# Two heads per round in a prompt attention, and the last six rounds of a bisection moved among the products of the next projection

## What is computed

```python
def mixer_ab(hn, attend, conv_buf, h0, w_in, w_out, ...):
    q, k, v, qi, ki, wi, g, xr = split_cols(hn @ w_in, AB_SPLITS)
    attn = attend(q, k, v, qi, ki, wi)                    # prompt: 4 blocks of 128 queries, 8 heads
    rg, new_buf, h_last = rglru_branch(g, xr, conv_buf, h0, ...)
    return jnp.concatenate([attn, rg], axis=-1) @ w_out, ...

# sample attention: the 256 best of 4097 keys by the indexer's scores, for each of 8 samples
idx, valid = select_topk(indexer_scores(qi, wi, ki_all), q_pos, k_pos, 256)
k_sel = jnp.where(in_past, ck[phys, off], ...)            # gathered from a paged cache
# recurrence: h = a * h + u with a = exp(log_a), u = sqrt(-expm1(2 * log_a)) * (i * xc)
```

## Time and profile before

| | |
|---|---|
| median of 3 runs | 1317.52 us (1314.84 to 1319.84) |
| the profiled execution's own time | 1317.3 us |
| its span, first to last instruction | 1315.6 us |
| busy: TensorE, weight loads, VectorE, ScalarE, POOL | 96%, 92%, 53%, 35%, 14% of the span |
| bisection with attention, first count to first product of the output projection | 208.84 to 277.94 us |
| output projection, to the last product | to 367.94 us |

### The profile page before, as it was taken

The page is one execution under the profiler, slowest core; times in us unless marked ns, Lnnn a source line. Parts: engine busy times, 40 slices in busy tenths (PEclk is TensorE's granted clock), DMA queues, the critical chain, the costliest instruction groups (busy, mean ns, idle before and its releaser), DMA issues.

```text
span 1315.6 us, 24604 instructions
## 1 busy us (share of the span) xinstructions
PE 1258.2 (96%) x10078; PEld 1215.9 (92%) x10078; DVE 701.9 (53%) x1286; ACT 465.9 (35%) x540; POOL 187.3 (14%) x281
## 2 busy tenths in 40 slices
PE   6999998888999999999999999999999999999995
PEld 5979994677999999999999999998999999999994
DVE  5468997765265555555323346535655555542223
ACT  5242327642143433434222244333543434331110
POOL 1001101234031111111000010042211111110000
PEclk9999999998999999999999999999999999999998
DMA  6654212022022222222222231211222222222211
GB/s 218 173 115 159 97 33 79 3 101 92 1 105 97 92 96 96 96 96 88 89 89 99 96 129 65 97 66 64 97 96 96 90 74 91 96 88 92 95 53 65
DMA packets 26595, 120.40 MB, mean 92 GB/s; under 512 B 7880, under 2 KB 9224, under 8 KB 14504
## 3 DMA queue, kind: packets, MB, share of 16 engines
q1 hardware_dynamic: 21784, 107.67, 23.8%
q0 software_dynamic: 2048, 10.54, 2.4%
q10 hardware_dynamic: 2704, 1.35, 0.3%
HBM read 115.94 MB, written 3.61 MB: 91 GB/s over the span
## 4 chain that ended last, share of the span: by engine, by line
PE 90%; DVE 6%; issue 2%; ACT 2%; POOL 0%; DMA 0%; another core or an unknown queue 0%; DVEq 0%; SPq 0%; ACTq 0%
PE ps L852 22%; PE ps L855 21%; PE ps L853 21%; PE ps L983 4%; PE ps L984 3%; PE ps L986 3%; PE ps L1250 2%; PE ps L932 2%; PE ps L1251 1%; PE ps L1253 1%; PE ps L869 1%; PE ps L916 1%; DVE xc L1498 1%; PE ps L1054 1%; PE ps L897 1%
## 5 line engine op out<-in xcount | busy, mean ns | idle before, releaser
L852 PE MATMUL ps<-xh,w_h 128*128 128x260 f32 x1664 | 437.5, 284 | 7.4 <-POOL xl L2001 7.4
L853 PE MATMUL ps<-xl,w_h 128*128 128x260 f32 x1664 | 436.0, 283 | 0.0
L855 PE MATMUL ps<-xh,w_l 128*128 128x260 f32 x1664 | 335.3, 283 | 0.0
L852 PEld LDWEIGHTS ps<-xh,w_h 128*128 128x128 f32 x1664 | 315.1, 189 | 8.3 <-issue 7.6
L853 PEld LDWEIGHTS ps<-xl,w_h 128*128 128x128 f32 x1664 | 314.5, 189 | 0.1
L1353 DVE TENSOR_TENSOR w_l<-w_raw,w_h 128x2048 fp32r<-128x2048 f32 (+1 forms) x94 | 212.7, 2263 | 160.1 <-ACT w_h L519 159.9
L855 PEld LDWEIGHTS ps<-xh,w_l 128*128 128x128 f32 x1664 | 257.3, 189 | 0.0
L519 ACT ACTIVATE w_h<-w_raw 128x2048 fp32r<-128x2048 f32 (+1 forms) x50 | 92.3, 1845 | 263.3 <-PE ps L855 213.4
L853 PE MATMUL ps<-hl,w_h 128*128 128x260 f32 x704 | 183.9, 282 | 0.0
L852 PE MATMUL ps<-hh,w_h 128*128 128x260 f32 x704 | 183.4, 282 | 0.0
L855 PE MATMUL ps<-hh,w_l 128*128 128x260 f32 x704 | 141.8, 283 | 0.0
(11 more groups left out here) (311 smaller groups left out, 1569.4 us busy)
## 6 DMA issues: line engine op xcount, KB each, us to landing
w_raw<-in_wstream SPq DMA_DIRECT2D x86, 1024.0 KB, 4.8
w_raw<-in_wstream SPq DMA_DIRECT2D x8, 768.0 KB, 4.4
res<-in_x_t SPq DMA_DIRECT2D x4, 520.0 KB, 7.1
out_y<-yt SPq DMA_DIRECT2D x8, 260.0 KB, 2.2
tab<-bias_by_distance SPq DMA_DIRECT2D x16, 128.0 KB
wor<-in_wstream SPq DMA_DIRECT2D x4, 512.0 KB, 6.0
wm<-in_sgu_w ACTq DMA_DIRECT2D x1, 512.0 KB, 3.6
sb_b<-in_sgu_b ACTq DMA_DIRECT2D x1, 512.0 KB, 4.1
```

The lines of the kernel that those rows point to most:

```text
L852: pe.matmul(out[h], wh, hi[h], start=(first and k == 0), stop=False)
L853: pe.matmul(out[h], wh, lo[h], start=False, stop=False)
L855: ins = pe.matmul(out[h], wl, hi[h], start=False, stop=(last and k == nk - 1))
```

## The change

It changes only orders. (1) Heads 16 to 31 have their logits two per round, in rounds 17 to 24. (2) `rg_share` moves to rounds 4 to 7, the square root to the place ahead of all exponentials, the scans to rounds 13 to 16, `rg_samples` to 17, `fill_high` to 21 to 24. (3) The split of slab 11 moves to round 14 on ScalarE and to round 20 on VectorE. (4) TensorE's counts of rounds 26 to 31 move behind steps 0, 2, 3, 5, 7 and 9 of the first slab (`LATE_ROUNDS`), with the last values at step 0, the last output transposes at 4, and everything of the selection and the sample attention some steps later. (5) On VectorE the last division comes after round 27, `attention_low` after round 30, the first slab's `add_half` ahead of the slot ranks' inputs, and the slot rows, `add_half` and the split of slab 12 are ordered anew.

```diff
-        for rnd in range(17, 33):
-            ROUND[rnd] = (rnd - 1,)
+        for rnd in range(17, 25):
+            ROUND[rnd] = (2 * rnd - 18, 2 * rnd - 17)
...
             act.wait_ge(ex_done, 4)
             act.wait_ge(th_done, 4)
-            act.wait_ge(slab_done, 10)
-            split(11, 1)
+            act.wait_ge(e_done, 4)
+            act.activation(th[:], th[:], ACT.Sqrt).then_inc(sqrt_done, 1)
...
-                if rnd == 17:
-                    roots()
-                if 29 <= rnd < 33:
-                    fill_high(1, rnd - 29, gg[:, rnd - 29, :], rg_done, rnd - 28)
+                if rnd == 14:
+                    act.wait_ge(slab_done, 10)
+                    split(11, 1)
+                if 21 <= rnd < 25:
+                    fill_high(1, rnd - 21, gg[:, rnd - 21, :], rg_done, rnd - 20)
...
-            for rnd in range(32):
+            for rnd in range(26):
                 count(rnd)
...
-                if n == 1:
+                if n == 0:
+                    p_work(26)
+                if n in LATE_ROUNDS:
+                    count(LATE_ROUNDS[n])
+                if n == 4:
+                    p_out(NCH - 1)
+                if n == 12:
                     tie_counts()
-                if n == 2:
-                    p_work(33)
-                if n == 4:
+                if n == 15:
                     chosen_before()
-                if n == 5:
-                    p_work(34)
-                if n == 7:
+                if n == 18:
                     for i in range(3):
                         slot_ranks(i)
-                    p_out(NCH - 1)
-                if 8 <= n < 21:
-                    slot_ranks(n - 5)
+                if 19 <= n < 32:
+                    slot_ranks(n - 16)
...
-                if n == 56:
+                if n == 60:
                     sample_rows()
...
-            p_work(32)
+            LATE_ROUNDS = {0: 26, 2: 27, 3: 28, 5: 29, 7: 30, 9: 31}
...
                 compare(rnd)
-                if 9 <= rnd < 13:
-                    rg_share(rnd - 9)
-                if rnd == 13:
+                if 4 <= rnd < 8:
+                    rg_share(rnd - 4)
+                if rnd == 8:
                     dve.wait_ge(e_done, 4)
                     dve.memset(atr[:, :, SEQ:T], 0.0)
+                if rnd == 20:
                     split(11, 1)
-                if 21 <= rnd < 25:
-                    rg_scan(rnd - 21)
-                if rnd == 25:
+                if 13 <= rnd < 17:
+                    rg_scan(rnd - 13)
+                if rnd == 17:
                     rg_samples()
...
                 decide(rnd)
+                if rnd == 27:
+                    p_divide(NCH - 1)
+                if rnd == 30:
+                    for j in range(4):
+                        attention_low(j)
...
-            p_logits(31)
...
+            add_half(0, 0)
+            add_half(0, 1)
             dve.wait_ge(base_mm, 1)
...
-            p_divide(NCH - 1)
...
-            for i in range(3):
+            for i in range(9):
                 slot_row(i)
-            for j in range(4):
-                attention_low(j)
-            for i in range(3, 11):
+            split_next(10)
+            slot_row(9)
+            add_half(1, 0)
+            for i in range(10, 16):
                 slot_row(i)
-            add_half(0, 0)
-            add_half(0, 1)
-            for i in range(11, 16):
-                slot_row(i)
+            add_half(1, 1)
             hot_buckets()
-            split_next(10)
-            add_half(1, 0)
-            add_half(1, 1)
```

More of the change, by code:

```diff
@@ L1188, in beside_out @@
                 n = 16 * g + step
-                if n == 1:
+                if n == 0:
[5 more added lines that the diff above has]
+                if n == 12:
                     tie_counts()
-                if n == 2:
-                    p_work(33)
-                if n == 4:
+                if n == 15:
                     chosen_before()
-                if n == 5:
-                    p_work(34)
-                if n == 7:
+                if n == 18:
                     for i in range(3):
                         slot_ranks(i)
-                    p_out(NCH - 1)
-                if 8 <= n < 21:
-                    slot_ranks(n - 5)
-                if n == 24:
+                if 19 <= n < 32:
+                    slot_ranks(n - 16)
+                if n == 34:
                     keys_turn(0)
-                if n == 25:
+                if n == 35:
                     hot_turn()
-                if n == 29:
+                if n == 37:
                     keys_turn(1)
-                if n == 31:
+                if n == 38:
                     sample_logits(0)
-                if n == 37:
+                if n == 44:
                     keys_turn(2)
-                if n == 44:
+                if n == 49:
                     keys_turn(3)
-                if n == 45:
+                if n == 50:
+                    sample_logits(1)
+                if n == 51:
                     weights_turn(0)
-                if n == 46:
-                    sample_logits(1)
-                if n == 47:
+                if n == 52:
                     sample_values(0)
-                if n == 51:
+                if n == 55:
                     weights_turn(1)
-                if n == 53:
+                if n == 57:
                     sample_values(1)
-                if n == 56:
+                if n == 60:
                     sample_rows()
@@ L1676, in p_divide, with attention_low, add_half @@
                    sumr[:, blk, :].rearrange("p (h a) -> p h a", a=1).broadcast_to((P, 8, 64)), ALU.mult).then_inc(ao_done, 1)
+            def attention_low(j):
+                dve.wait_ge(at_ev, NCH)
+                dve.wait_ge(x_lo, 12)
+                dve.wait_ge(x_hi, 13 + j)
+                tt(xl[:, 4 + j, :], atr[:, j, :], xh[:, 4 + j, :].bitcast(F32), ALU.subtract).then_inc(x_lo, 1)
+            def add_half(g, t):
+                dve.wait_ge(half_done if t == 0 else slab_done, 10 + g + 1)
+                for h in range(2):
+                    r = res[:, 2 * g + t, h * HT:(h + 1) * HT]
+                    ins = tt(r, ps[:, 2 * t + h, 0:HT], r, ALU.add)
+                ins.then_inc(half_added if t == 0 else b_free, 1)
             key_halves()
@@ L1747, in slot_row @@
                     tt(row2[:, four], grow[:, four], gab[:, four, 0], ALU.add).then_inc(rows2_done, 1)
-            def attention_low(j):
-                dve.wait_ge(at_ev, NCH)
-                dve.wait_ge(x_lo, 12)
-                dve.wait_ge(x_hi, 13 + j)
-                tt(xl[:, 4 + j, :], atr[:, j, :], xh[:, 4 + j, :].bitcast(F32), ALU.subtract).then_inc(x_lo, 1)
             def hot_buckets():
@@ L1761, in hot_buckets @@
                 tt(hot_b[:], dge[:, :, 1:33], dge[:, :, 0:32], ALU.subtract).then_inc(hot_done, 1)
-            def add_half(g, t):
-                dve.wait_ge(half_done if t == 0 else slab_done, 10 + g + 1)
-                for h in range(2):
-                    r = res[:, 2 * g + t, h * HT:(h + 1) * HT]
-                    ins = tt(r, ps[:, 2 * t + h, 0:HT], r, ALU.add)
-                ins.then_inc(half_added if t == 0 else b_free, 1)
             def sample_least(n):
```

3 lines of the change are left out of this document (removed).

## The result

The changed kernel takes 1329.2 us (median of 4 runs, 1326.5 to 1331.4); the kernel before took 1318.4 beside it. The ratio is 1.0085, its 95% interval 1.0064 to 1.0106: slower, where the forecast was 1310.5. The profiled execution, the longest of the four (1331.4), spans 1329.6 us, 14.0 more than before.

The account below looks back on a forecast made before the run. TensorE, nine tenths of the chain of waits, was taken as the bound. Gains of 2.9, 0.4 and 5.3 make 8.6, less 1.7 for half clock: 1317.3 - 6.9 = 1310.4, say 1310.5 us; range 1303 to 1319.

Parts of the forecast that it names:

- the term of the table load: Rounds 4 to 9: the root's own load, bounds 0 and 1.28 us, taken as 0; head 0's exponential 2.3 late.
- two terms of the sum: Rounds 10 to 16: some 5.5 us from head 0's exponential to head 8's logits; scan waiting for rates, head 8 1.6 late.
- VectorE is the bound at 2.5 per round: Rounds 10 to 16 after head 8: VectorE sets the pace, 2.5 us per round, 4.4 in round 15.
- the waits of the divisions: Rounds 17 to 25: divisions of blocks 1 and 2 ahead of logits, with round 20's split, leave TensorE 2.5 us idle.
- The first slab: Output projection's first slab: waits 10.9 us before, 5.05 after, counts 0.6, so 5.3 gained.
- The rest: Gathers of keys, samples' output rows and SyncE's slab loads move at no cost; 1 to 2 us without cover.
- The signal with no engine behind it: End of the first slab: VectorE's 2.35 us standing, within the 4.48 wait, let go; its return kept as a bound.
- The wait at the key turns: Behind the first slab: a wait at the key turns was named as a sign that the forecast is wrong.
- POOL: Rounds 10 to 13: its multiplication slows threshold updates, up to 0.6 us in each of three rounds; taken as 0.
- C: Rival: new waits keep TensorE at 1.2 GHz from step 3 to 23 of the projection; 1323.2, up to 1326; chance 0.12.
- B: Rival, gain eaten: root's load waits (1.28), the 2.35 returns, one more half-clock stretch (1.5); 1315.5 us; chance 0.16.
- D: Rival: pair rounds stay a three-engine loop, about 4.7 us each, eight rounds; slab gains as forecast; 1317.4 us; chance 0.08.

Follow-up runs that it names:

- i1: h2 with the root back in round 17, shares in rounds 9 to 12 and scans behind the logits in rounds 20 and 21; 1314.7 us.
- h2: g2 without its filling products in rounds 4 to 13 (those of the changed kernel stay); 1309.9 us, ratio 0.9942 to the kernel before.
- g2: f2 with g1's order, the hot turn a step later and filling products (results thrown away) in rounds 4 to 13; 1312.5 us.
- f2: The changed kernel with e2's later scans and e3's wait ahead of the ninth gather together; 1315.9 us.
- g1: The changed kernel with the divisions of blocks 0 to 2 and VectorE's half of slab 11's split behind the logits and decision; 1326.0 us.
- f1: The changed kernel with more products whose result is thrown away, in TensorE's gaps of rounds 4 to 13; 1326.9 us.
- e2: The changed kernel with the four scans in rounds 17 to 20, the samples' step in 21 and the fills two rounds later; 1322.5 us.
- e3: The changed kernel with POOL waiting for the hot buckets ahead of the ninth gather; 1322.4 us.

## Why the prediction was wrong

**Rounds 4 to 9: the term of the table load.** The last share ended 9.6 us after the first count, as forecast. The root's own load I put at the lower of its bounds, 0, and it took the upper, 1.28: it stands behind the wait for the shares in ScalarE's order, though ScalarE had been idle 3.15 us. Head 0's exponential at 221.71 looks like the forecast's 221.7, but this execution's loop began 1.36 earlier; it is 1.4 late. By the Trainium skill, ScalarE: Activation LUTs, section "What ACT_TABLE_LOAD costs", 1.38 us of drain were to come with each load; as before, none shows (root 0.01 us after the load, load 0.02 after the root).

**Rounds 10 to 16: two terms of the sum.** I took 5.5 us from head 0's exponential to head 8's logits without the split and the shares. With the split gone, i1 has 7.4, and h2, without shares or scans in these rounds, 8.9 (7.95 in g2, where the clock stays full): most of what I subtracted from the 8.66 had been hidden. The scan's wait for the rates then came on top, at 24.7 after the first count instead of 19.8, and "VectorE is the bound at 2.5 per round" failed with it: the scan is ahead of the logits in a loop over three engines. The place was right (the prediction named the wait), its size was not: head 8 was 6.5 late where I had 1.6.

**Rounds 17 to 25: the waits of the divisions.** TensorE is the bound, as forecast, and its work without waits is 33.2 us from head 16's logits (h2), where I had 30.7 (0.9, 29.4 and 0.4). For the divisions and the split I took 2.5; f2 against h2 shows 3.55, since a late second head also runs by itself, 0.91, instead of together with the first. Block 2's division brought half clock besides (0.72 over 6 us), and with it g1 against the changed kernel shows 4.8.

**The first slab: right.** Waits of 0.78, 0.99, 0.54 and 0.91 for the forecast 1.05, 1.15, 0.9 and 1.05, at full clock, so even the 1.0 set aside for half clock was not needed.

**The rest: the step that failed most.** The gathers were costed at nothing, 1 to 2 us without cover. By the profiles they cost 9 to 10 (99.2 against 90.1 and 88.8), by the medians 6.8 to 11.3, with the half clock behind them; where that ended sooner the same sixteen gathers left 93.5 (f1). The cover that I looked at was not what failed: the first gather was issued 13.7 us ahead of the first turn of keys, 8.6 closer than before where I had 3, and the turn did not wait for it. What failed is that the gathers were put down as transfers alone, at no cost to the other engines. The signal with no engine behind it was in the rows, and so were the gathers before, which had pauses; I treated it as part of a wait that would go, with its 2.35 us as the bound. ScalarE's timeline of the kernel before has the same sign:

```profile
303.14 1.91 ACT L519 ACTIVATE w_h<-w_raw 128x2048 fp32r<-128x2048 f32 x1 [12.89 <-remote]
```

This split could start when the first slab was done, at about 300.1. It and the slot row at 303.18 both began within 0.2 us of the end of the eighth gather in a row (303.06). The wait at the key turns that I named as a sign came (0.36, and 1.59 at the hot turn). With slot rows that now come without a pause, the gathers lost theirs.

**POOL** beside rounds 10 to 13: a threshold update took 0.70 where POOL multiplied, and ScalarE was awaited there anyway; 0 was right.

**The rivals.** C gave the sign and came nearest to the time, by a mechanism that did not happen: the clock in the slab stayed full from 283.8 to 324. B's load came true. Of D's eight rounds of 4.7, three lasted about that long or longer. No rival had the gathers in it. With the same work done, taking out one loss does not bring the run back into the range: it is at 1322.5 with the scans later (e2) and at 1322.4 with the pause (e3). With both it is at 1315.9 (f2). That h2's 1309.9 is close to the forecast is partly luck: it is another kernel, still has the table load's 1.4, and its two stretches (67.5 and 86.7) lie 1.3 above and 0.8 under the 66.2 and 87.5 of the sum.

## What to carry to other kernels

In a loop over several engines, work that nobody awaits in the same round belongs behind the step that others wait for; costed as filling an engine's spare time, it is paid again as a late partner on the engine that sets the pace. A wait that the profile puts down to no engine is a cost to place, not one to drop: ask which stream of transfers runs beside it and what the change does to that stream's pauses. Before filling gaps to hold up a clock, see whether the stretch at the lower level is on the path at all.

## What the runs showed of the hardware

Sixteen indirect gathers in a row (0.95 us each, 0.3 apart, 21 us in all) kept ScalarE from an instruction that was ready for 8.6 us, and it went on 1.8 to 2.2 us after the last one's issue in four kernels; a pause of 6.1 us in the middle, or plain loads of the same size with pauses of 1.2 to 3.7 us, removed that. Eight in a row were felt too: 3.0 us on ScalarE and 2.35 on VectorE in the kernel before, 0.91 on VectorE in e3. By the Trainium skill, Runtime: NRT & Kernel Launch, section "Instruction fetch mechanics", each sequencer fetches its instructions in blocks of 16 KiB over a DMA queue of its own, mostly hidden; this trace has such a queue (43 packets with 0.70 MB, 16 KB each), but no run here shows that it was a fetch that the gathers held. Between 318 and 340 us the changed kernel moved one packet on it, in the microsecond from 323, and none near 331.8, when ScalarE went on.

Two heads' score products on 64 rows each (384 columns) took 0.94 to 1.49 us queued together, and 0.91 each when the second came late.
